# Placing the SBUF buffers of a two-block transformer kernel from both ends of the memory

## The chip, the core and the metric

The kernel runs on one core of one Trainium2 chip. The metric is the device time of the core in microseconds, from the first to the last instruction and what lies around them. Weights and inputs lie in HBM; the on-chip memory (SBUF) has 128 partitions, and every buffer of the kernel takes the same range of byte addresses in each of them. In this text an address is the byte offset within a partition.

## What is computed

Two residual blocks of two layers each act on x of 256 tokens by 1024 channels, all in float32. Cut to what matters:

```python
def first_block(x, ...):
    for l in range(DEPTH):                      # 2 layers
        h = rms_norm(x, attn_norm_g[l])
        pa, pb, pc = split(h @ w_in[l])         # RWKV-7, dilated and latent attention
        x = x + concat([ya, yb, yc]) @ w_out[l] # 1024 x 1024
        h = rms_norm(x, ffn_norm_g[l])
        x = x + (silu(h @ w_gate[l]) * (h @ w_up[l])) @ w_down[l]   # 1024 x 2816
    return rms_norm(x, final_norm_g)

def second_block(x, mem, ...):
    for l in range(DEPTH):                      # 2 layers
        proj = rms_norm_2(x, norm_g[l]) @ w_in[l]
        ...                                     # stick-breaking, MoBA, memory attention
        mkv = rms_norm_2(mem, mem_norm_g[l]) @ w_mem_kv[l]
        x = x + concat([o_sb, o_mb, o_mem]) @ w_out[l]
    return rms_norm_2(x, final_norm_g)
```

## The kernel before

The residual x is kept on chip with channels on partitions, as `x_res` (8 tiles of 128 channels by 256 tokens). Weights come from HBM as 132 chunks of 1 MB (128 partitions by 2048 floats), in the order of use, through the two halves of `w_raw`. Each product of a float32 weight with a float32 activation is made of three matmuls in the format float32r: the weight w is split into `w_hi` (rounded by ScalarE, L269) and `w_lo` = w minus w_hi (VectorE, L275), the activation in the same way (`act_hi`/`act_lo` for the normed x, `mixed_hi`/`mixed_lo` and `gated_hi`/`gated_lo` in the first block, `mem_hi`/`mem_lo` in the second), and the result is hi·HI + hi·LO + lo·HI. All these matmuls have a stationary operand of 128 columns and a moving operand of 256 columns; each loads its stationary operand anew. A chunk makes 48 of them, so there are 132 x 48 = 6336.

In nearly all of them the weight split is the stationary operand and the activation is the moving one, as in the gate and up projections of the feed-forward stage:

```python
TE.matmul(o, hi[:, w], HI[:, k, :], start=(k == 0 and x == 0), stop=False)
TE.matmul(o, hi[:, w], LO[:, k, :], start=False, stop=False)
last = TE.matmul(o, lo[:, w], HI[:, k, :], start=False, stop=(k == KT - 1 and x == 1))
```

Lines of the profile: L1120 to L1122 (input projections, first block), L1146 to L1148 (output projection, moving `mixed_*`), L1889 to L1891 (gate and up), L1911 to L1913 (down, moving `gated_*`), L2109 to L2111 (input projections, second block; in the two chunks of the memory's keys and values the activations are `mem_*`), L2141 to L2143 (output projection, moving `mem_*`). In some chunks the roles are turned, with w_hi or w_lo moving: L1125 to L1127 and L2114 to L2116.

By moving buffer: `act_*` or the weights with act stationary, 4320 matmuls; `gated_*` 528 in each layer; `mixed_*` 384; the memory's projections and the second block's output projection, with `mem_*`, 192 + 384 = 576.

The work runs in stages, one after the other: start, mixers of layer 0, feed-forward of layer 0, mixers of layer 1, feed-forward of layer 1, then the two layers of the second block. In each stage every engine has its own instruction list written out by hand; engines meet at semaphores. In the feed-forward stages TensorE's list is nearly only the matmuls above. In the mixer stages small matmuls of the attention and of the recurrence stand between the chunks.

SBUF buffers come from an allocator that stacks: each `K.sb(...)` takes the next free address, and leaving its context gives it back. Before the change all are stacked upwards from the low end, in the order of the calls; 16,512 bytes at the bottom are taken by the runtime and constants.

Of the kernel before, what the change touches and what calls it, by code (L numbers as in the profile page):

```python
# [28 lines left out]
fp32 = mybir.dt.float32  # L29
# [147 lines left out]
class Stream:  # L177
# [7 lines left out]
    def __init__(self, K):  # L185
        self.K, self.nc = K, K.nc
        raw = K.sb("w_raw", [P, 2, CHUNK])
# [105 lines left out]
class Kernel:  # L293
# [3 lines left out]
    def __init__(self, nc, ctx, io):  # L297
        self.nc, self.ctx, self.io = nc, ctx, io
        self.sems, self.total, self.base, self.named = {}, {}, {}, {}
        self.X = self.sb("x_res", [P, KT, T])  # L300
        self.HI = self.sb("act_hi", [P, KT, T], f32r)
        self.LO = self.sb("act_lo", [P, KT, T], f32r)
        self.PRMS = self.sb("prm", [P, WIDTH["prm"] + N_PRMS])
        self.st = Stream(self)
        self.SQ = self.sb("squares", [P, 3, 512])
        self.RSALL = self.sb("norm_rs", [P, T + NT])
        self.RSB, self.RS = self.RSALL[:, 0:T], self.RSALL[:, T:T + NT]
        self.cst_sb = {"both": self.sb("consts_both", [P, WIDTH["both"]]), "prm": self.PRMS}
# [2478 lines left out]
def program(nc, io, out):  # L2787
    with ExitStack() as ctx:
        K = Kernel(nc, ctx, io)
        GAINS = K.sb("gains", [P, KT])  # L2790
        block = ctx.enter_context(nc.Block())
        first, second = {}, {}
        with ExitStack() as c:
            norm = Norm(K, 0, 0, K.prm(Q_G, KT))
            first["rope_tables"] = K.sb("rope_tables", [P, 4, T], c=c)
            first["positions"] = K.sb("positions", [P, T], i32, c)[:, :]
# [4 lines left out]
            K.cst_sb["first"] = K.sb("consts_first", [P, WIDTH["first"]], c=c)  # L2801
# [13 lines left out]
        with ExitStack() as c:  # L2815
            K.cst_sb["second"] = K.sb("consts_second", [P, WIDTH["second"]], c=c)
            second["mem"] = K.sb("mem", [P, KT, T], c=c)[:, :, :]
            second["gates"] = K.sb("gates", [P, 8, T], c=c)
            second["mem_tokens"] = second["gates"].rearrange("p (t x) c -> p t (x c)", t=NT)
            second["mem_rs_row"] = K.sb("mem_rs_row", [P, T], c=c)  # L2820
            second["mem_ss"] = K.sb("mem_ss", [P, NT], c=c)
            second["mem_rs"] = K.sb("mem_rs", [P, NT], c=c)
            SQ2 = K.sb("scaled_squares", [P, 3, 512], c=c)
            R1 = K.sb("first_rs", [P, T + NT], c=c)
# [123 lines left out]
```

How the kernel before makes its waits and increments, by code:

```python
    def sync(self, name=None):  # L168
        name = name or self.own
        self.eng.wait_ge(self.K.sem(name), self.K.total[name])
# [43 lines left out]
    def split_quarter_hi(self, act, g, q):  # L214
        if q == 0:
            act.wait_ge(self.K.sem("quarters_in0" if g else "quarter_in"), 16)
        else:
            act.wait_ge(self.K.sem(f"quarters_in{q}"), 32)
        self.nc.scalar.activation(self.quarter(self.split[g][0], q), self.quarter(self.raw[g], q),
                                  ACT.Copy).then_inc(self.K.sem("quarter_hi"), 1)
# [1 line left out]
    def split_quarter_lo(self, dve, g, q):  # L222
        dve.wait_ge(self.K.sem("quarter_hi"), 2 * q + g + 1)
        hi, lo = (self.quarter(x, q) for x in self.split[g])
        self.nc.vector.tensor_tensor(lo, self.quarter(self.raw[g], q), hi.bitcast(fp32),
                                     ALU.subtract).then_inc(self.K.sem("quarter_lo"), 1)
# [1 line left out]
    def quarter_arrived(self, pe, g, q):  # L228
        pe.wait_ge(self.K.sem("quarter_lo"), 2 * q + g + 1)
# [12 lines left out]
    def load(self, sp, i):  # L242
        g = self.first + i
        if g >= len(self.src):
            return
        if g == 3:
            sp.wait_ge(self.K.sem("quarter_hi"), 2)
            sp.dma_start(self.raw_slot(g), self.src[g]).then_inc(self.K.sem("quarters_in0"), 16)
            return
        if g in (4, 5):
            sp.wait_ge(self.K.sem("quarter_hi"), g + 3)
            sp.wait_ge(self.K.sem("quarter_lo"), g + 3)
        elif g > 5:
            sp.wait_ge(self.hi_ready, self.ready(g - self.RAW, 1))
```

## Time and profile before

| | us |
|---|---|
| median of 3 runs | 969.79 (964.67 to 973.5) |
| profiled execution, its own time | 969.01 |
| profiled execution, span of its instructions | 967.2 |
| TensorE matmul busy | 937.9 (97%) |
| TensorE weight load busy | 886.4 (92%) |
| VectorE busy | 680.7 (70%) |
| ScalarE busy | 554.6 (57%) |
| DMA, mean rate over the span | 155 GB/s |

Matmuls overlap in the pipeline and their ends are modelled, so what matters of them is how far apart they start, not how long each is shown. The granted clock of TensorE is at 1.00 of 2.4 GHz in nearly every stretch.

### The profile page before, as it was taken

The numbers are of one execution on the slowest core, as the hardware profiler recorded it, in microseconds if no ns is written. First come the engines' busy times: TensorE is split into PE (matmuls) and PEld (weight loads), VectorE is DVE, ScalarE is ACT, GpSimd is POOL, SyncE is SP. The second block draws the span as 40 slices with busy tenths as digits, with TensorE's granted clock in tenths as the row PEclk, the third lists the DMA queues.
The fourth block names the chain that finished last, engine by engine and source line by source line (L and its number), as shares of the span: only waits on it lengthen the run. The fifth ranks groups of instructions, "written<-read, shape, count | busy, mean of one in ns | idle before, by whom it ended". The sixth has DMA issues, their size and how long they took to land.

```text
span 967.2 us, 20420 instructions
## 1 busy us (share of the span) xinstructions
PE 937.9 (97%) x8862; PEld 886.4 (92%) x8862; DVE 680.7 (70%) x972; ACT 554.6 (57%) x851; POOL 7.6 (1%) x12
## 2 busy tenths in 40 slices
PE   8899999999999999999999999999999999999996
PEld 7788799999999988878999999998899899999896
DVE  6898666866744679966776666348699677698674
ACT  6873466645443578355654444337487666486565
POOL 0000000000000001000000000000000000000000
PEclk9999999999999999999999999999999999999999
DMA  9341115565555433211466654554353335453241
GB/s 337 159 165 55 46 58 194 205 228 210 180 194 198 175 128 135 89 46 46 155 218 229 242 189 174 185 199 140 131 175 131 94 137 189 149 174 135 94 141 69
DMA packets 23145, 149.89 MB, mean 155 GB/s; under 512 B 2576, under 2 KB 2832, under 8 KB 6032
## 3 DMA queue, kind: packets, MB, share of 16 engines
q1 hardware_dynamic: 23056, 148.59, 43.2%
q8 instruction: 70, 1.15, 0.5%
q14 instruction: 19, 0.16, 0.0%
HBM read 147.26 MB, written 1.05 MB: 153 GB/s over the span
## 4 chain that ended last, share of the span: by engine, by line
PE 68%; DVE 18%; ACT 9%; issue 2%; DMA 1%; SPq 0%; DVEq 0%; ACTq 0%
PE bank L1889 8%; PE bank L1890 8%; PE bank L1891 8%; DVE w_lo L275 6%; PE bank L2109 4%; PE bank L1912 4%; PE bank L1911 4%; PE bank L1913 4%; ACT w_hi L269 3%; PE bank L2110 3%; PE bank L2111 3%; PE bank L2114 2%; PE bank L2116 2%; PE bank L2115 2%; ACT act_hi L372 1%
## 5 line engine op out<-in xcount | busy, mean ns | idle before, releaser
L275 DVE TENSOR_TENSOR w_lo<-w_raw,w_hi 128x1024 fp32r<-128x1024 f32 x256 | 306.4, 1225 | 108.5 <-ACT w_hi L269 107.6
L269 ACT ACTIVATE w_hi<-w_raw 128x1024 fp32r<-128x1024 f32 x256 | 259.5, 1053 | 209.0 <-PE bank L1891 103.3
L1889 PE MATMUL bank<-act_hi,w_hi 128*128 128x256 f32 x704 | 196.7, 279 | 1.6 <-DVE w_lo L275 1.0
L1890 PE MATMUL bank<-act_lo,w_hi 128*128 128x256 f32 x704 | 195.9, 278 | 0.0
L1891 PE MATMUL bank<-act_hi,w_lo 128*128 128x256 f32 x704 | 195.9, 278 | 0.0
L1889 PEld LDWEIGHTS bank<-act_hi,w_hi 128*128 128x128 f32 x704 | 133.5, 190 | 2.4 <-issue 1.4
L1890 PEld LDWEIGHTS bank<-act_lo,w_hi 128*128 128x128 f32 x704 | 132.2, 188 | 0.1
L1891 PEld LDWEIGHTS bank<-act_hi,w_lo 128*128 128x128 f32 x704 | 132.1, 188 | 0.0
L2109 PE MATMUL bank<-act_hi,w_hi 128*128 128x256 f32 x352 | 100.7, 286 | 3.9 <-DVE w_lo L275 2.4
L1912 PE MATMUL bank<-gated_lo,w_hi 128*128 128x256 f32 x352 | 98.7, 280 | 0.0
L1911 PE MATMUL bank<-gated_hi,w_hi 128*128 128x256 f32 x352 | 98.5, 280 | 0.0
L1913 PE MATMUL bank<-gated_hi,w_lo 128*128 128x256 f32 x352 | 98.5, 280 | 0.0
L2110 PE MATMUL bank<-act_lo,w_hi 128*128 128x256 f32 x352 | 97.8, 278 | 0.0
L2111 PE MATMUL bank<-act_hi,w_lo 128*128 128x256 f32 x352 | 97.8, 278 | 0.0
L1120 PE MATMUL bank<-act_hi,w_hi 128*128 128x256 f32 x256 | 75.0, 293 | 4.2 <-DVE w_lo L275 2.2
L2109 PEld LDWEIGHTS bank<-act_hi,w_hi 128*128 128x128 f32 x352 | 66.4, 189 | 6.9 <-DVE w_lo L275 3.4
L1122 PE MATMUL bank<-act_hi,w_lo 128*128 128x256 f32 x256 | 71.2, 278 | 0.0
L1121 PE MATMUL bank<-act_lo,w_hi 128*128 128x256 f32 x256 | 71.2, 278 | 0.0
L1911 PEld LDWEIGHTS bank<-gated_hi,w_hi 128*128 128x128 f32 x352 | 66.3, 188 | 0.0
L1912 PEld LDWEIGHTS bank<-gated_lo,w_hi 128*128 128x128 f32 x352 | 66.2, 188 | 0.0
L2110 PEld LDWEIGHTS bank<-act_lo,w_hi 128*128 128x128 f32 x352 | 66.2, 188 | 0.1
L2111 PEld LDWEIGHTS bank<-act_hi,w_lo 128*128 128x128 f32 x352 | 66.2, 188 | 0.0
(370 smaller groups left out, 1994.7 us busy)
## 6 DMA issues: line engine op xcount, KB each, us to landing
w_raw<-in_w_ffn SPq DMA_DIRECT2D x66, 1024.0 KB, 4.8
w_raw<-in_w_mix SPq DMA_DIRECT2D x62, 1024.0 KB, 4.9
small_w<-in_small SPq DMA_DIRECT2D x2, 1280.0 KB, 7.5
w_raw<-in_w_mix SPq DMA_DIRECT2D x8, 256.0 KB, 6.0
x_res<-in_x_channels SPq DMA_DIRECT2D x4, 256.0 KB, 5.6
probs<-in_w_mix SPq DMA_DIRECT2D x2, 512.0 KB, 7.5
probsT<-in_w_mix SPq DMA_DIRECT2D x1, 1024.0 KB, 10.2
mem<-in_mem_channels SPq DMA_DIRECT2D x1, 1024.0 KB, 7.4
```

Source lines behind the costliest of these rows:

```text
L269: self.nc.scalar.activation(hi, self.piece(self.raw_slot(g), p), ACT.Copy).then_inc(self.hi_ready, 1)
L275: self.nc.vector.tensor_tensor(lo, self.piece(self.raw_slot(g), p), hi.bitcast(fp32), ALU.subtract).then_inc(self.lo_ready, 1)
L1120: TE.matmul(o, hi[:, w], HI[:, k, :], start=(k == 0 and x == 0), stop=False)
L1889: TE.matmul(o, hi[:, w], HI[:, k, :], start=(k == 0 and x == 0), stop=False)
L1890: TE.matmul(o, hi[:, w], LO[:, k, :], start=False, stop=False)
L1891: last = TE.matmul(o, lo[:, w], HI[:, k, :], start=False, stop=(k == KT - 1 and x == 1))
L1911: TE.matmul(out, hi[:, w], GHI[:, k, :], start=(k == 0 and o % 2 == 0), stop=False)
L1912: TE.matmul(out, hi[:, w], GLO[:, k, :], start=False, stop=False)
L1913: last = TE.matmul(out, lo[:, w], GHI[:, k, :], start=False, stop=(k == FK - 1 and o % 2 == 1))
L2109: TE.matmul(o, hi[:, w], h[:, k, :], start=(k == 0 and x == 0), stop=False)
L2110: TE.matmul(o, hi[:, w], l[:, k, :], start=False, stop=False)
L2111: last = TE.matmul(o, lo[:, w], h[:, k, :], start=False, stop=(k == KT - 1 and x == 1))
```

## The change

The allocator is asked for two stacks: `K.sb(..., top=True)` takes its buffer from the high end of the memory downwards, all others from the low end upwards. On top go `x_res`, `prm`, `w_raw`, `squares`, `norm_rs`, `consts_*`, `gains`, `rope_tables`, `positions`, and of the second block `mem`, `gates`, `mem_rs_row`, `mem_ss`, `mem_rs`, `scaled_squares` and `first_rs`. At the low end stay `act_hi`/`act_lo`, `w_hi`/`w_lo`, `mixed_*`, `gated_*`, `mem_hi`/`mem_lo` and the buffers of the mixers.

```diff
-        raw = K.sb("w_raw", [P, 2, CHUNK])
+        raw = K.sb("w_raw", [P, 2, CHUNK], top=True)
         hi, lo = K.sb("w_hi", [P, 2, CHUNK], f32r), K.sb("w_lo", [P, 2, CHUNK], f32r)
...
-        self.X = self.sb("x_res", [P, KT, T])
         self.HI = self.sb("act_hi", [P, KT, T], f32r)
         self.LO = self.sb("act_lo", [P, KT, T], f32r)
-        self.PRMS = self.sb("prm", [P, WIDTH["prm"] + N_PRMS])
+        self.X = self.sb("x_res", [P, KT, T], top=True)
+        self.PRMS = self.sb("prm", [P, WIDTH["prm"] + N_PRMS], top=True)
         self.st = Stream(self)
-        self.SQ = self.sb("squares", [P, 3, 512])
-        self.RSALL = self.sb("norm_rs", [P, T + NT])
+        self.SQ = self.sb("squares", [P, 3, 512], top=True)
+        self.RSALL = self.sb("norm_rs", [P, T + NT], top=True)
...
-    def sb(self, name, shape, dt=fp32, c=None):
+    def sb(self, name, shape, dt=fp32, c=None, top=False):
...
-        return (c or self.ctx).enter_context(self.nc.sbuf_tensor(name, shape, dt))
+        return (c or self.ctx).enter_context(
+            self.nc.sbuf_tensor(name, shape, dt, side="right" if top else "left"))
...
-            K.cst_sb["second"] = K.sb("consts_second", [P, WIDTH["second"]], c=c)
-            second["mem"] = K.sb("mem", [P, KT, T], c=c)[:, :, :]
-            second["gates"] = K.sb("gates", [P, 8, T], c=c)
+            K.cst_sb["second"] = K.sb("consts_second", [P, WIDTH["second"]], c=c, top=True)
+            second["mem"] = K.sb("mem", [P, KT, T], c=c, top=True)[:, :, :]
+            second["gates"] = K.sb("gates", [P, 8, T], c=c, top=True)
```

No instruction is added, removed or moved: on every engine the list is the same, and so are all waits. Only addresses differ. The allocator aligns to 32 bytes; adding up the buffers' sizes gives these start addresses (all in bytes; the last two columns are the remainder on division by 512, before and after):

| buffer | size | before | after | mod 512 | mod 512 |
|---|---|---|---|---|---|
| act_hi | 8192 | 24704 | 16512 | 128 | 128 |
| act_lo | 8192 | 32896 | 24704 | 128 | 128 |
| w_hi | 16384 | 58560 | 32896 | 192 | 128 |
| w_lo | 16384 | 74944 | 49280 | 192 | 128 |
| mixed_hi | 8192 | 106240 | 65664 | 256 | 128 |
| mixed_lo | 8192 | 114432 | 73856 | 256 | 128 |
| gated_hi, layer 0 | 22528 | 131328 | 83072 | 256 | 128 |
| gated_lo, layer 0 | 22528 | 153856 | 105600 | 256 | 128 |
| gated_hi, layer 1 | 22528 | 131424 | 65664 | 352 | 128 |
| gated_lo, layer 1 | 22528 | 153952 | 88192 | 352 | 128 |
| mem_hi | 8192 | 131424 | 65664 | 352 | 128 |
| mem_lo | 8192 | 139616 | 73856 | 352 | 128 |
| w_raw | 16384 | 42176 | 203680 | 192 | 416 |
| x_res | 8192 | 16512 | 221152 | 128 | 480 |

Tiles within these buffers lie 512 or 1024 bytes apart, so they share the remainder.

## Rows read from the trace of the kernel before

**Rows 1.** Page, part 1: busy time, share of the span, instructions
```profile
PE 937.9 (97%) x8862; PEld 886.4 (92%) x8862; DVE 680.7 (70%) x972; ACT 554.6 (57%) x851; POOL 7.6 (1%) x12
```
**Rows 2.** Page, part 4: the chain that ended last, by engine
```profile
PE 68%; DVE 18%; ACT 9%; issue 2%; DMA 1%; SPq 0%; DVEq 0%; ACTq 0%
```
**Rows 3.** Windows: mixers 0, feed-forward 0 and 1, second block's layer 0
```profile
7.00:150.20 143.20, 135.73 (x1651) 120.01 (x1652) 113.97 (x201) 88.93 (x159) 3.68 (x4) 1.00 0.36 134
150.20:334.50 184.30, 183.51 (x1593) 183.08 (x1592) 115.96 (x128) 88.35 (x103) 0.00 (x0) 1.00 0.55 198
...
474.00:662.50 188.50, 187.71 (x1592) 187.29 (x1591) 115.52 (x127) 89.95 (x107) 0.00 (x0) 1.00 0.56 200
662.50:812.20 149.70, 144.98 (x1182) 135.46 (x1181) 117.11 (x176) 101.08 (x167) 0.00 (x0) 1.00 0.41 141
```
**Rows 4.** Timeline of PE (start us, us): gate/up, layer 0, 48 matmuls apart
```profile
261.43 0.28 PE L1889 MATMUL bank<-act_hi,w_hi 128*128 128x256 f32 x1
...
266.87 0.28 PE L1889 MATMUL bank<-act_hi,w_hi 128*128 128x256 f32 x1
```
**Rows 5.** Timeline of PE: gate/up, layer 1, 48 matmuls apart
```profile
537.74 0.28 PE L1889 MATMUL bank<-act_hi,w_hi 128*128 128x256 f32 x1
...
543.39 0.28 PE L1889 MATMUL bank<-act_hi,w_hi 128*128 128x256 f32 x1
```
**Rows 6.** Timeline of PE, gate/up to down, layer 0: 6, then 42 matmuls apart
```profile
271.63 0.28 PE L1889 MATMUL bank<-act_hi,w_hi 128*128 128x256 f32 x1
...
272.31 0.28 PE L1911 MATMUL bank<-gated_hi,w_hi 128*128 128x256 f32 x1
...
277.25 0.28 PE L1911 MATMUL bank<-gated_hi,w_hi 128*128 128x256 f32 x1
```
**Rows 7.** Timeline of PE: down, layer 1, 48 matmuls apart
```profile
624.84 0.28 PE L1911 MATMUL bank<-gated_hi,w_hi 128*128 128x256 f32 x1
...
630.54 0.28 PE L1911 MATMUL bank<-gated_hi,w_hi 128*128 128x256 f32 x1
```
**Rows 8.** Timeline of PE: output projection of the first block, 48 matmuls apart
```profile
139.12 0.28 PE L1148 MATMUL bank<-mixed_hi,w_lo 128*128 128x256 f32 x1
...
144.78 0.28 PE L1148 MATMUL bank<-mixed_hi,w_lo 128*128 128x256 f32 x1
```
**Rows 9.** Timeline of PE: output projection of the second block, 48 matmuls apart
```profile
950.17 0.28 PE L2141 MATMUL bank<-mem_hi,w_hi 128*128 128x256 f32 x1
...
955.88 0.28 PE L2141 MATMUL bank<-mem_hi,w_hi 128*128 128x256 f32 x1
```
**Rows 10.** Timeline of PE: weights moving, act stationary, 45 matmuls apart
```profile
706.19 0.28 PE L2114 MATMUL bank<-w_hi,act_hi 128*128 128x256 f32 x1
...
711.29 0.28 PE L2114 MATMUL bank<-w_hi,act_hi 128*128 128x256 f32 x1
```
**Rows 11.** Timeline of PE: weights moving, mem stationary, 24 matmuls apart
```profile
888.46 0.28 PE L2114 MATMUL bank<-w_hi,mem_hi 128*128 128x256 f32 x1
...
891.34 0.28 PE L2114 MATMUL bank<-w_hi,mem_hi 128*128 128x256 f32 x1
```
**Rows 12.** Groups by line, window 218.2:256.2 (gate/up, layer 0)
```profile
L1890 PE MATMUL bank<-act_lo,w_hi 128*128 128x256 f32 x113 | 31.2, 276 | 0.0
```
**Rows 13.** Groups by line, window 548.9:599.7 (gate/up, layer 1)
```profile
L1890 PE MATMUL bank<-act_lo,w_hi 128*128 128x256 f32 x145 | 40.7, 281 | 0.0
```
**Rows 14.** Page, part 5: three groups whose moving operand is act
```profile
L1891 PE MATMUL bank<-act_hi,w_lo 128*128 128x256 f32 x704 | 195.9, 278 | 0.0
...
L2111 PE MATMUL bank<-act_hi,w_lo 128*128 128x256 f32 x352 | 97.8, 278 | 0.0
...
L1122 PE MATMUL bank<-act_hi,w_lo 128*128 128x256 f32 x256 | 71.2, 278 | 0.0
```
**Rows 15.** Timeline of PE: 16 transposes in a row, other operands and form
```profile
932.47 1.91 PE L567 MATMUL bank<-consts_both,probs 128*128 128x128 f32 x16
```
**Rows 16.** Groups by line, VectorE: one shape at three places
```profile
L1933 DVE TENSOR_TENSOR gated<-up,gate 128x512 f32<-128x512 f32 x22 | 15.2, 692 | 1.2 <-ACT gate L1927 0.5
...
L394 DVE TENSOR_TENSOR squares<-squares 128x512 f32<-128x512 f32 x21 | 14.4, 688 | 0.7
```
**Rows 17.** Page, part 6: the weight chunks' transfers
```profile
w_raw<-in_w_ffn SPq DMA_DIRECT2D x66, 1024.0 KB, 4.8
```

More of the change, by code:

```diff
@@ L299, in __init__ @@
         self.sems, self.total, self.base, self.named = {}, {}, {}, {}
[L300 removed]
         self.HI = self.sb("act_hi", [P, KT, T], f32r)
         self.LO = self.sb("act_lo", [P, KT, T], f32r)
[L303 removed]
+        self.X = self.sb("x_res", [P, KT, T], top=True)
+        self.PRMS = self.sb("prm", [P, WIDTH["prm"] + N_PRMS], top=True)
         self.st = Stream(self)
[L305 to L306 removed]
+        self.SQ = self.sb("squares", [P, 3, 512], top=True)
+        self.RSALL = self.sb("norm_rs", [P, T + NT], top=True)
         self.RSB, self.RS = self.RSALL[:, 0:T], self.RSALL[:, T:T + NT]
[L308 removed]
+        self.cst_sb = {"both": self.sb("consts_both", [P, WIDTH["both"]], top=True), "prm": self.PRMS}
         self.PS = ctx.enter_context(nc.psum_tensor("bank", [P, 8 * 512], fp32))
         self.banks = [self.PS[:, 512 * i:512 * (i + 1)] for i in range(8)]
[L312 removed]
+    def sb(self, name, shape, dt=fp32, c=None, top=False):
         self.named[name] = self.named.get(name, -1) + 1
         name = f"{name}_{self.named[name]}" if c else name
[L315 removed]
+        return (c or self.ctx).enter_context(
+            self.nc.sbuf_tensor(name, shape, dt, side="right" if top else "left"))
     def sem(self, name):
@@ L2789, in program @@
         K = Kernel(nc, ctx, io)
-        GAINS = K.sb("gains", [P, KT])
+        GAINS = K.sb("gains", [P, KT], top=True)
         block = ctx.enter_context(nc.Block())
@@ L2794, in program @@
             norm = Norm(K, 0, 0, K.prm(Q_G, KT))
-            first["rope_tables"] = K.sb("rope_tables", [P, 4, T], c=c)
-            first["positions"] = K.sb("positions", [P, T], i32, c)[:, :]
+            first["rope_tables"] = K.sb("rope_tables", [P, 4, T], c=c, top=True)
+            first["positions"] = K.sb("positions", [P, T], i32, c=c, top=True)[:, :]
             with ExitStack() as shared:
@@ L2800, in program @@
             K.sb("small_w_end", [P, N_SMALL + 4 * T - 2 * KT * T], c=c)
-            K.cst_sb["first"] = K.sb("consts_first", [P, WIDTH["first"]], c=c)
+            K.cst_sb["first"] = K.sb("consts_first", [P, WIDTH["first"]], c=c, top=True)
             stage_start(K, block, norm, GAINS[:, :], first)
@@ L2815, in program @@
         with ExitStack() as c:
-            K.cst_sb["second"] = K.sb("consts_second", [P, WIDTH["second"]], c=c)
-            second["mem"] = K.sb("mem", [P, KT, T], c=c)[:, :, :]
-            second["gates"] = K.sb("gates", [P, 8, T], c=c)
+            K.cst_sb["second"] = K.sb("consts_second", [P, WIDTH["second"]], c=c, top=True)
+            second["mem"] = K.sb("mem", [P, KT, T], c=c, top=True)[:, :, :]
+            second["gates"] = K.sb("gates", [P, 8, T], c=c, top=True)
             second["mem_tokens"] = second["gates"].rearrange("p (t x) c -> p t (x c)", t=NT)
[L2820 to L2824, printed above, removed]
+            second["mem_rs_row"] = K.sb("mem_rs_row", [P, T], c=c, top=True)
+            second["mem_ss"] = K.sb("mem_ss", [P, NT], c=c, top=True)
+            second["mem_rs"] = K.sb("mem_rs", [P, NT], c=c, top=True)
+            SQ2 = K.sb("scaled_squares", [P, 3, 512], c=c, top=True)
+            R1 = K.sb("first_rs", [P, T + NT], c=c, top=True)
             chunk = DEPTH * (N_MIX1 + N_FFN)
```

## Prediction

> **What bounds the kernel now.** I began with the busy times: TensorE 97%, its weight loads 92%, VectorE 70%, ScalarE 57% [rows 1], and the chain that ended last is 68% TensorE [rows 2]. By stage, the two feed-forward stages (184.3 and 188.5 us) are filled to 99% by weight loads; the mixer stage shown has 84% and the second block's layer 90% [rows 3]. So what decides is how far apart TensorE's matmuls start. The change moves no instruction. It can act only if an address changes how long something takes, so the question put to the trace is: do equal matmuls on different buffers start at different distances?
>
> They do. All rows below are of one form (128 columns stationary, 256 moving), without a wait between them, at the full granted clock:
>
> - moving `act_*`, layer 0: 5.44 us for 48, or 113.3 ns [rows 4];
> - the same code on the same addresses in layer 1: 5.65 us for 48, 117.7 ns [rows 5];
> - moving `gated_*`, layer 0: 0.68 us for the 6 up to the border, 113.3 ns; 4.94 us for the 42 after it, 117.6 ns [rows 6]. The distance changes with the first matmul that reads `gated_hi`, with no wait there;
> - moving `mixed_*`: 5.66 us for 48, 117.9 ns [rows 8];
> - moving `gated_*` in layer 1, at a start 96 bytes off: 5.70 us for 48, 118.8 ns [rows 7];
> - moving `mem_*`: 5.71 us for 48, 119.0 ns [rows 9];
> - moving weights on stationary act: 5.10 us for 45, 113.3 ns [rows 10]; on stationary `mem_*`: 2.88 us for 24, 120.0 ns [rows 11].
>
> I read two things out of this. First, a stream can run in a fast beat (113.3) or a slow one (117.7) on the same addresses; something at its start picks one, and it keeps it. Second, `gated_*`, `mixed_*` and `mem_*` were never seen in the fast beat over a longer stretch, and `act_*` and the weights were. The buffers that can be fast all lie under 91,400; the others from 106,240 up. They also differ in the remainder by 512 (128 and 192 against 256 and 352), so the trace can't say whether height or remainder counts. The change puts every moving buffer at remainder 128, that of act, and all but a part of layer 0's `gated_*` (up to 128,128) under 111,000. By both readings it goes the same way.
>
> How often is act slow? A matmul is shown with 276 ns in the fast stretch [rows 12] and 281 in the slow one [rows 13]. The groups over the whole span give 195.9 / 704 = 278.3, 97.8 / 352 = 277.8 and 71.2 / 256 = 278.1 ns [rows 14], so 45%, 37% and 42% slow: I take 43%.
>
> **The change part by part.** Against 113.3 ns, what the 6336 matmuls now lose:
>
> 1. `gated_*`, layer 0: 528 x 4.4 = 2.3 us [rows 6].
> 2. `gated_*`, layer 1: 528 x 5.5 = 2.9 us [rows 7].
> 3. `mixed_*`: 384 x 4.6 = 1.8 us [rows 8].
> 4. `mem_*`, 576 x 5.7 = 3.3 us [rows 9].
> 5. act, slow 43% of the time: 4320 x 0.43 x 4.4 = 8.2 us [rows 5, 14].
>
> Together 18.5 us, 10.3 of it in the first four. The likeliest result is that after the change these four behave as act does, fast more than half of the time: they then still lose 2016 x 0.43 x 4.4 = 3.8 us, so 6.5 us are gained. Terms 1 to 3 lie in stretches that TensorE fills; term 4 lies in a stage filled to 90% [rows 3], where part is lost to waits for other engines. I take 0.9 of the whole: 5.9 us. Term 5 stays, as the beat is picked anew in each execution; it can differ by some 4 us a stage (22 chunks x 48 x 4.4 ns = 4.6 us), which is also the size of the spread of the three runs.
>
> Other engines' operations, with their operands at new places (`w_raw`, `x_res`, `squares`, constants): no trace shows them up there. One shape of VectorE takes 688 ns on `squares` (from 91,328) and 692 ns on `gate`/`up`/`gated` (from 176,384) [rows 16], 0.6% apart. On the 680.7 us of VectorE [rows 1] that is at most 4 us either way, and spread over an engine 30% idle: I take 0, with 1 us to both sides. The transfers into `w_raw` land in 4.8 us [rows 17] against 5.44 us in which a chunk is used up [rows 4]; they stay hidden. If they became slower by over 0.6 us each in the feed-forward stages, they would come to bound them; nothing in the trace ties their time to an address, so I price it at nothing.
>
> Sum on the profiled execution's own time: 969.0 - 5.9 = **963 us**. The median of the runs is 0.8 us above that execution, which I leave out.
>
> The Trainium skill speaks against any effect. "SBUF — State Buffer", in "Who interferes with whom", says that TensorE never waits on anyone, and "TensorE: Matmul & The Clock Gate", in its step on LDWEIGHTS, that loading the next weights takes no read bandwidth from the running matmul, since the two have ports of their own. By these rules equal matmuls take equal time wherever they read, and the time would stay at 969. The rows do not agree: 113.3 against 117.6 ns across a border with no wait [rows 6]. The second page also gives a spacing of columns over 2.4 GHz plus 2.5 ns, which would be 109.2 ns here; no stretch of these matmuls in this trace reaches it.
>
> **The rivals.**
>
> *All fast.* The remainders of the moving and the stationary operand become equal (128 and 128; now 128 against 192 for act), and if that takes away the meeting of the two read streams that makes the slow beat, all 6336 run at 113.3: 18.5 x 0.9 = 16.7 us gained, 952. For it: operands 32 bytes off a multiple of 64 are the slowest [rows 7, 9, 11], so finer alignment helps. Against it: no row shows that equal remainders are better than the present 64 bytes apart. It could go further: transposes of another form start 109 ns apart ((1.91 - 0.27) / 15) [rows 15]; with all at 109 the gain would be 6336 x 7.2 x 0.9 = 41 us, 928. That is the outermost bound.
>
> *Slower: the two streams meet in each matmul.* The same equal remainder can be the bad one. The stationary operand of the next matmul is loaded while the moving one is read; if both walk through the same part of the memory from the same remainder, each matmul pays. Price: the worst stretch seen, 120.0 ns [rows 11]. The mean now is 113.3 + 18.5 / 6336 = 116.2 ns, so (120.0 - 116.2) x 6336 x 0.9 = 22 us: 991. It decides from a mean above 116.2. A milder form is that only the slow beat is left: 4320 x 0.57 x 4.4 = 10.8 us lost, 528 x 1.1 + 576 x 1.3 = 1.3 us gained, times 0.9: 978.
>
> *No effect of the address.* Then `gated_*` and `mixed_*` were slow for another reason, such as the order in which output banks are written, and 969 stays. Against it: in the last two chunks of each such product the output stays on one half bank for 12 matmuls, longer than in gate and up, and a chunk of that kind ran in the slow beat too [rows 8].
>
> **How the numbers follow.** As act is now: 0.40, 963 (its own range 957 to 969). All fast: 0.31, 952, with a thin tail to 928. No effect: 0.11, 969. Slow beat only: 0.09, 978. Meeting in each matmul: 0.09, 991. About 1% (9.7 us) is what a measurement of this kernel can tell from no change. Faster by over 1% (under 960): all fast, and the lower edge of the first case: 0.35. Slower by over 1% (over 979.5): the last case and half of the one before: 0.15. Between: 0.50. The range is 946 to 983: it leaves out the last case and the tail of the second.
>
> **What would show each step.** In the profile after: L1911 to L1913, L1146 to L1148 and L2141 to L2143 have stretches of 48 matmuls in 5.44 us; their shown mean falls from 280 to about 278. Layer 1's feed-forward comes within one beat difference of layer 0's, since the 96-byte offset is gone. VectorE's L275 stays within 1% of 1225 ns and the raw chunks land in 4.8 us. The prediction is wrong if the spacing of `act_*` itself changes to a value that is neither 113.3 nor 117.7, because then the relation of the two operands, which I hold to be without effect, decides; or if L275 and L269 at their new places change by several per cent.

## The result and the profile after

| | before | after |
|---|---|---|
| median of 4 runs, us | 971.29 (964.67 to 973.5) | 984.83 (984.68 to 985.7) |
| profiled execution, span, us | 967.2 | 982.9 |

The ratio after to before is 1.0147, with a 95% interval from 1.0111 to 1.0183: slower by about 14 us. (One run more of the kernel before than in its own section: 972.79.) The forecast was 963, and 984.8 lies just outside the range of 946 to 983. One more thing has changed: the runs after lie within 1.0 us of each other, those of before within 8.8 us.

The page of the profile after: busy times, the chain that ended last, and four of its groups of instructions and transfers. From L378 of before on its line numbers are those of before plus 2.

```profile
PE 960.7 (98%) x8862; PEld 910.1 (93%) x8862; DVE 681.2 (69%) x972; ACT 554.5 (56%) x851; POOL 7.6 (1%) x12
...
PE 73%; DVE 15%; ACT 7%; issue 2%; DMA 1%; SPq 0%; DVEq 0%; ACTq 0%
...
L275 DVE TENSOR_TENSOR w_lo<-w_raw,w_hi 128x1024 fp32r<-128x1024 f32 x256 | 306.3, 1225 | 107.6 <-ACT w_hi L269 106.6
...
L1893 PE MATMUL bank<-act_hi,w_lo 128*128 128x256 f32 x704 | 199.2, 283 | 0.0
...
L1893 PEld LDWEIGHTS bank<-act_hi,w_lo 128*128 128x128 f32 x704 | 135.1, 192 | 0.0
...
w_raw<-in_w_ffn SPq DMA_DIRECT2D x66, 1024.0 KB, 4.8
```

Only TensorE has more busy time: 960.7 against 937.9 us for its matmuls, 910.1 against 886.4 us for its weight loads [rows 1]. VectorE (681.2 against 680.7) and ScalarE (554.5 against 554.6) stand still, the split of the weights reads `w_raw` from its new place in the same 1225 ns (the line of before is below), and its transfers land in the same 4.8 us [rows 17]. The chain has moved from VectorE to TensorE, 73% against 68% [rows 2]. So nothing shows a cost at the buffers that went to the top, and what costs is in the matmuls. L1893, with 199.2 us against 195.9, is shown with 283 ns, a duration that neither the fast nor the slow stretches of before have (276 and 281) [rows 12 to 14].

```profile
L275 DVE TENSOR_TENSOR w_lo<-w_raw,w_hi 128x1024 fp32r<-128x1024 f32 x256 | 306.4, 1225 | 108.5 <-ACT w_hi L269 107.6
```

By stage (mixers 0, feed-forward 0 and 1, the second block's layer 0; columns as in [rows 3]: the stretch and its length, the busy times of TensorE's matmuls, its weight loads, VectorE, ScalarE and GpSimd with their counts, the granted clock, the share of the DMA engines and GB/s):

```profile
7.00:150.90 143.90, 139.15 (x1651) 123.11 (x1650) 114.11 (x202) 88.60 (x158) 3.67 (x4) 0.99 0.36 133
150.90:342.60 191.70, 191.29 (x1591) 190.95 (x1591) 115.95 (x128) 88.29 (x103) 0.00 (x0) 1.00 0.52 191
482.40:674.20 191.80, 191.39 (x1593) 191.05 (x1592) 115.56 (x127) 89.91 (x107) 0.00 (x0) 1.00 0.54 196
674.20:825.90 151.70, 147.65 (x1180) 138.68 (x1180) 117.40 (x176) 101.06 (x167) 0.00 (x0) 1.00 0.40 140
```

Against [rows 3] the mixers are 0.7 us longer, the two feed-forward stages 7.4 and 3.3 us, the second block's layer 2.0 us. Before, the two feed-forward stages differed by 4.2 us; now they are equal. The granted clock is 1.00 in three of the four stages and 0.99 in the mixers, where before had 1.00 in all four, so the clock is not the reason.

The timeline of TensorE after, in pairs of rows 48 matmuls apart (the last pair 45): gate and up of layer 0, gate and up of layer 1, down of layer 1, output projection of the mixers 0, output projection at the very end, and a chunk of the second block in which `w_hi` moves and act is stationary.

```profile
261.12 0.28 PE L1891 MATMUL bank<-act_hi,w_hi 128*128 128x256 f32 x1
...
266.88 0.28 PE L1891 MATMUL bank<-act_hi,w_hi 128*128 128x256 f32 x1
...
537.82 0.28 PE L1893 MATMUL bank<-act_hi,w_lo 128*128 128x256 f32 x1
...
543.58 0.28 PE L1893 MATMUL bank<-act_hi,w_lo 128*128 128x256 f32 x1
...
624.82 0.28 PE L1914 MATMUL bank<-gated_lo,w_hi 128*128 128x256 f32 x1
...
630.58 0.28 PE L1914 MATMUL bank<-gated_lo,w_hi 128*128 128x256 f32 x1
...
139.82 0.28 PE L1150 MATMUL bank<-mixed_hi,w_lo 128*128 128x256 f32 x1
...
145.58 0.28 PE L1150 MATMUL bank<-mixed_hi,w_lo 128*128 128x256 f32 x1
...
964.94 0.28 PE L2145 MATMUL bank<-mem_hi,w_lo 128*128 128x256 f32 x1
...
970.70 0.28 PE L2145 MATMUL bank<-mem_hi,w_lo 128*128 128x256 f32 x1
...
718.83 0.28 PE L2116 MATMUL bank<-w_hi,act_hi 128*128 128x256 f32 x1
...
724.23 0.28 PE L2116 MATMUL bank<-w_hi,act_hi 128*128 128x256 f32 x1
```

Five times 5.76 us for 48, and 5.40 us for 45: 120.0 ns in each. Before, the same places had 113.3 or 117.7 (act), 118.8, 117.9, 119.0 and 113.3 [rows 4, 5, 7 to 10]. Everything runs in one beat, whatever the moving buffer, and it is the spacing that of the streams shown before only the worst had [rows 11].

### The profile page after: what moved, and what is told of

Its sections match the earlier page's. It is cut to its first block, busy times and chain, and to the rows that moved or that the text cites. A ratio compares the mean times of both kernels' runs of the same rounds, so it can differ in the third digit from the quotient of the medians.

```text
span 982.9 us, 20420 instructions
## 1 busy us (share of the span) xinstructions
PE 960.7 (98%) x8862; PEld 910.1 (93%) x8862; DVE 681.2 (69%) x972; ACT 554.5 (56%) x851; POOL 7.6 (1%) x12
## 4 chain that ended last, share of the span: by engine, by line
PE 73%; DVE 15%; ACT 7%; issue 2%; DMA 1%; SPq 0%; DVEq 0%; ACTq 0%
PE bank L1891 8%; PE bank L1892 8%; PE bank L1893 8%; DVE w_lo L275 5%; PE bank L2111 4%; PE bank L2112 4%; PE bank L2113 4%; PE bank L1915 4%; PE bank L1914 4%; PE bank L1913 4%; ACT w_hi L269 3%; PE bank L2116 2%; PE bank L2118 2%; PE bank L2117 2%; PE bank L569 1%
## 5 line engine op out<-in xcount | busy, mean ns | idle before, releaser
L269 ACT ACTIVATE w_hi<-w_raw 128x1024 fp32r<-128x1024 f32 x256 | 259.2, 1052 | 218.0 <-PE bank L1893 115.6
L275 DVE TENSOR_TENSOR w_lo<-w_raw,w_hi 128x1024 fp32r<-128x1024 f32 x256 | 306.3, 1225 | 107.6 <-ACT w_hi L269 106.6
L1891 PE MATMUL bank<-act_hi,w_hi 128*128 128x256 f32 x704 | 199.9, 284 | 0.8 <-DVE w_lo L275 0.8
L1892 PE MATMUL bank<-act_lo,w_hi 128*128 128x256 f32 x704 | 199.2, 283 | 0.0
L1893 PE MATMUL bank<-act_hi,w_lo 128*128 128x256 f32 x704 | 199.2, 283 | 0.0
L1891 PEld LDWEIGHTS bank<-act_hi,w_hi 128*128 128x128 f32 x704 | 135.1, 192 | 1.5 <-issue 1.2
L1892 PEld LDWEIGHTS bank<-act_lo,w_hi 128*128 128x128 f32 x704 | 135.1, 192 | 0.1
L1893 PEld LDWEIGHTS bank<-act_hi,w_lo 128*128 128x128 f32 x704 | 135.1, 192 | 0.0
L2111 PE MATMUL bank<-act_hi,w_hi 128*128 128x256 f32 x352 | 102.1, 290 | 3.2 <-DVE w_lo L275 2.2
L2112 PE MATMUL bank<-act_lo,w_hi 128*128 128x256 f32 x352 | 99.5, 283 | 0.0
L2113 PE MATMUL bank<-act_hi,w_lo 128*128 128x256 f32 x352 | 99.5, 283 | 0.0
L1122 PE MATMUL bank<-act_hi,w_hi 128*128 128x256 f32 x256 | 76.3, 298 | 2.1 <-DVE w_lo L275 1.4
L2111 PEld LDWEIGHTS bank<-act_hi,w_hi 128*128 128x128 f32 x352 | 67.3, 191 | 6.0 <-DVE w_lo L275 3.3
L1123 PE MATMUL bank<-act_lo,w_hi 128*128 128x256 f32 x256 | 72.4, 283 | 0.0
L1124 PE MATMUL bank<-act_hi,w_lo 128*128 128x256 f32 x256 | 72.3, 283 | 0.0
L1915 PEld LDWEIGHTS bank<-gated_hi,w_lo 128*128 128x128 f32 x352 | 67.6, 192 | 0.0
L2112 PEld LDWEIGHTS bank<-act_lo,w_hi 128*128 128x128 f32 x352 | 67.4, 191 | 0.1
```

The source lines that it names most:

```text
L269: self.nc.scalar.activation(hi, self.piece(self.raw_slot(g), p), ACT.Copy).then_inc(self.hi_ready, 1)
L275: self.nc.vector.tensor_tensor(lo, self.piece(self.raw_slot(g), p), hi.bitcast(fp32), ALU.subtract).then_inc(self.lo_ready, 1)
L1915: last = TE.matmul(out, lo[:, w], GHI[:, k, :], start=False, stop=(k == FK - 1 and o % 2 == 1))
L2111: TE.matmul(o, hi[:, w], h[:, k, :], start=(k == 0 and x == 0), stop=False)
L2112: TE.matmul(o, hi[:, w], l[:, k, :], start=False, stop=False)
L2113: last = TE.matmul(o, lo[:, w], h[:, k, :], start=False, stop=(k == KT - 1 and x == 1))
```

## The experiments

Two words are needed in what follows. The **distance** of a matmul is the address of its moving operand minus that of its stationary one, modulo 256 bytes. I write "act on w" for act moving and the weights stationary. Before, act on w has distance 192, `gated_*` of layer 0 and `mixed_*` 64, `gated_*` of layer 1 and `mem_*` 160, weights moving on act 64, weights moving on `mem_*` 96. After, all have 0. Wherever a spacing is given, it is the mean time from start to start in a stretch without a wait; where the single steps alternate, it moves by 0.1 or 0.2 ns with the stretch chosen. For the whole kernel I also use the **loss**: the sum over its unbroken pairs of such matmuls of what their spacing has above 113.33 ns. It is 18.2 us before and 40.7 us after.

### The new places with the old remainders, and the old places with equal remainders

First kernel: the changed one, with gaps that give every operand back its old remainder by 512 while it stays at its new height.

```diff
         self.LO = self.sb("act_lo", [P, KT, T], f32r)
...
+        self.sb("gap_w", [P, 16])
         self.st = Stream(self)
+        self.sb("gap_moving", [P, 16])
...
+            K.sb("gap_second", [P, 24], c=c)
             K.cst_sb["second"] = K.sb("consts_second", [P, WIDTH["second"]], c=c, top=True)
```

> The changed kernel with three gaps (64 bytes ahead of w_hi, 64 bytes behind w_lo, 96 bytes ahead of the second block's buffers), so that every buffer stays at its new place from both ends, but the weight splits and moving operands have the remainders by 512 that they had before (act 128, w 192, mixed and gated of layer 0 256, gated of layer 1 and mem 352). Theory R (the remainder between moving and stationary operand sets the spacing of the matmuls): back to the time of before, 965 to 973 us, act in beats of 113.3 or 117.7 ns, gated 117.7 and 118.7. Theory P (the new places themselves cost, by height or through w_raw, x_res and the constants at the top): stays at 985, spacing 120.0 everywhere.

Measured: 970.63 us (10 runs) against 969.16 for the kernel before (13 runs), ratio 1.0002 [0.997, 1.0033]; loss 16.5 us. The rows of its groups:

```profile
L1894 PE MATMUL bank<-act_lo,w_hi 128*128 128x256 f32 x704 | 195.9, 278 | 0.0
L1895 PE MATMUL bank<-act_hi,w_lo 128*128 128x256 f32 x704 | 195.9, 278 | 0.0
```

195.9 us is the number of the kernel before [rows 14]. Gaps of 64, 64 and 96 bytes in memory that nothing uses give the whole 14 us back.

Second kernel: the one before, all stacked from the low end, with `prm` behind the weight buffers and gaps, so that every operand has the same remainder.

```diff
-        self.PRMS = self.sb("prm", [P, WIDTH["prm"] + N_PRMS])
         self.st = Stream(self)
+        self.PRMS = self.sb("prm", [P, WIDTH["prm"] + N_PRMS])
...
+            K.sb("gap_first", [P, 96], c=c)
...
+            K.sb("gap_second", [P, 72], c=c)
```

> The kernel before with prm moved behind w_lo and two gaps (384 and 288 bytes), so that all buffers stay stacked from the low end within a few hundred bytes of their old places, but act, w, mixed, gated and mem all have the remainder 128 by 512. Theory R: 983 to 987 us, spacing 120.0 ns for all 6336 matmuls. Theory P: 965 to 973 us, spacings as before.

Measured: 985.81 us (985.36 to 985.98, 4 runs), ratio 1.0158 [1.0102, 1.0214]; loss 40.7 us, the very number of after, and 120.0 ns in every stream.

```profile
L1890 PE MATMUL bank<-act_lo,w_hi 128*128 128x256 f32 x704 | 199.2, 283 | 0.0
L1891 PE MATMUL bank<-act_hi,w_lo 128*128 128x256 f32 x704 | 199.2, 283 | 0.0
```

With that the result is explained down to the low bits of the addresses: the remainders are all of it, and height and the two stacks show no effect (to 0.3%, the interval of the first pair; the last pair of kernels below agrees to 0.1 us). What it is in the remainders, the next two kernels ask.

### Matmuls alone: the distance, then the height

A kernel of nothing but the matmuls of a chunk (output: a copy of x). All operands lie in one buffer `big`. A group is 48 matmuls in the order of the gate and up projections; three groups are run at each distance, and TensorE waits for ScalarE between them. LO has the remainder of HI, w_lo that of w_hi.

```python
for m, st in CONFIGS:                   # addresses of HI and w_hi
    ...
    for r in range(GROUPS):
        ...
        for k in range(8):
            for x in range(2):
                ...                     # the slices of big
                TE.matmul(o, hi, HI, ...)
                TE.matmul(o, hi, LO, ...)
                last = TE.matmul(o, lo, HI, ...)
        g += 1
        last.then_inc(s["pe"], 1)
        pe.wait_ge(s["go"], g)
```

> Not the reference's work: only float32r matmuls (128 columns stationary, 256 moving, the order hi.HI, hi.LO, lo.HI of the kernel) on one big buffer, 24 settings of the distance moving minus stationary, three runs of 48 matmuls for each with a wait between them; the output is a copy of x. Both operands lie under 70,000. Distances modulo 1024: 0, 16, 32, 48, 64, 96, ... 480, 512, 576, 768, 960, then 0 and 64 again. Theory R: distance 0 gives 120.0 ns in all three runs; 64 and 448 (960) give 113.3 or 117.7 by run; distances that are not a multiple of 64 give 118 to 121; a multiple of 512 is as 0, and I have no forecast for 128, 256 and 384 (if the period is 128, all three as 0). Theory P: no spacing depends on the distance, all of 113 to 118 as both operands are low.

Measured (ns; where groups at one distance differ, all values seen; the first group of all, whose first matmuls start 213 ns apart, is counted in none of these kernels):

| distance | spacing | distance | spacing |
|---|---|---|---|
| 0, 256, 512, 768 | 120.0 | 128, 384 | 118.7, once 120.0 |
| 16 | 117.3 | 160 | 117.3 to 118.7 |
| 32 | 116.7 to 117.8 | 192, 448, 960 | 113.3 |
| 48 | 116.7 | 224, 480 | 118.3 |
| 64, 320, 576 | 117.8, 117.8, 113.3 | 288 | 116.7 to 117.8 |
| 96, 352 | 120.0 | 416 | 117.3 to 118.7 |

The first two rows below have distance 0, the last two distance 192; each pair is 30 matmuls apart:

```profile
43.71 0.28 PE L76 MATMUL bank<-big 128*128 128x256 f32 x1
...
47.31 0.28 PE L76 MATMUL bank<-big 128*128 128x256 f32 x1
...
194.31 0.28 PE L76 MATMUL bank<-big 128*128 128x256 f32 x1
...
197.71 0.28 PE L76 MATMUL bank<-big 128*128 128x256 f32 x1
```

3.60 us is 120.0 ns each, 3.40 us is 113.3 ns. The pattern repeats after 256 bytes. It also fits the streams of the trace of before: act at 192 in the fast beat (the slow one was not seen here, but is below), weights moving on act at 64 with 113.3 [rows 10], `gated_*` and `mixed_*` at 64 with 117.6 and 117.9, `mem_*` at 160 with 119.0, weights moving on `mem_*` at 96 with 120.0 [rows 6, 8, 9, 11]. What the slow beat is, it doesn't say.

> As the other measuring kernel, not the reference's work. Distances 0, 64 and 960 modulo 1024, each with moving/stationary operand near 17,500/37,000, 106,600/58,500, 131,200/58,500, 131,200/169,000 and 37,000/131,200; then distance 64 and 960 with the moving operand at remainders 0, 64, 160 and 256 by 1024; last the old place and remainder of gated (131,328 against 58,560). Theory R: the three groups of five differ, within a group all are alike: 120.0 for distance 0 and 113.3 or 117.7 for the others, wherever they lie; the absolute remainder is without effect except 160. Theory P with height: moving operands over 100,000 run at 117.7 or more, those at 17,500 reach 113.3, whatever the distance.

The same kernel at five places for both operands (moving at 17,536, 36,992, 106,624 and twice 131,200; stationary between 36,992 and 169,088) for each of three distances, then other remainders of the moving operand at distances 64 and 192. Measured: distance 0 gives 120.0 at all five places; 64 gives 117.8, 117.8, 113.3 at all five; 192 gives 113.3 at all five. Moving operands at remainders 0, 64 and 160 by 256 show no other values either. So, as long as LO has the remainder of HI and w_lo that of w_hi, only the distance of the two counts, and neither the height nor where one of them lies by itself. At distance 64 the group at 113.3 is nearly always the same: the third of its setting in 13 of the 14 settings of both kernels, always behind ScalarE's copy of 76 columns, and another group only once. So the start has a say in it.

### Every moving activation at distance 192

If 192 is the fast distance, `gated_*`, `mixed_*` and `mem_*` should get it as well: once with the old places, once with the new. (The matmuls with weights moving then all have 64.)

```diff
+            K.sb("gap_first", [P, 32], c=c)
...
+            K.sb("gap_second", [P, 8], c=c)
```

> The kernel before with two gaps only (128 bytes ahead of rope_tables, 32 bytes ahead of consts_second): act and w stay where they were, and mixed, gated and mem get a distance to w of -64 modulo 256, the one that act has. The measuring kernel ran this distance at 113.3 ns in all its runs, in every place. Theory R: mixed, gated and mem mostly at 113.3 instead of 117.7 to 119.0 ns; at most 10.3 us gained, less where act's slow beat (43% of its time before) is carried over: 959 to 966 us against 969. Theory P (high operands are slow): no change.

```diff
+        self.sb("gap_w", [P, 16])
         self.st = Stream(self)
+        self.sb("gap_moving", [P, 48])
```

> The changed kernel with two gaps (64 bytes ahead of w_hi, 192 bytes behind w_lo), so that all moving operands have the distance -64 modulo 256 to w, at the new places. Theory R: the same time as the kernel with this distance at the old places, within 0.5%, 959 to 966 us: 20 us less than the changed kernel as it is. If low operands or the top places give anything of their own, the two differ.

Measured: 966.22 (12 runs), ratio 0.9986 [0.9959, 1.0013], and 970.97 (12 runs), ratio 1.0027 [1.0003, 1.0051]. I had expected 959 to 966. Neither is a gain over the kernel before. But the single runs come in steps. Old places: 960.65, 961.34, 961.51; six from 965.6 to 967.2 and two near 968; 972.44. New places: three from 965.3 to 966.9, nine from 970.5 to 971.9. The two profiled executions lie on different steps. Old places (the two feed-forward stages of a 961.34 run):

```profile
150.60:333.00 182.40, 181.11 (x1592) 180.69 (x1591) 116.16 (x128) 88.24 (x103) 0.00 (x0) 1.00 0.55 200
472.10:654.90 182.80, 181.58 (x1592) 181.16 (x1591) 115.33 (x127) 89.21 (x106) 0.00 (x0) 1.00 0.56 206
```

The mean spacing is 113.5 and 113.8 ns in these stages, `gated_*` included. New places (the groups of a 971.79 run):

```profile
L1895 PE MATMUL bank<-act_hi,w_lo 128*128 128x256 f32 x704 | 197.4, 280 | 0.0
L1894 PE MATMUL bank<-act_lo,w_hi 128*128 128x256 f32 x704 | 197.3, 280 | 0.0
...
L1916 PE MATMUL bank<-gated_lo,w_hi 128*128 128x256 f32 x352 | 98.9, 281 | 0.0
```

Here both stages run at 117.4 ns on the average, 188.5 us each. At distance 192 a stage can have either beat for nearly its whole length, and that is worth 6 us a stage. The first kernel of the experiments speaks for a new draw in each execution: it has the remainders of before, but in its trace layer 0's feed-forward stage is the slow one (188.1 us) and layer 1's the fast one (184.1), the other way round from [rows 3]. The steps of some 5 us between runs are of this size, so this is very likely where the spread of the kernel before comes from; only one execution of each kernel has a trace. That the average over runs gains so little fits too: in both traces the buffers that came to 192 are fast or slow together with act.

The traces also show where the beat changes. The feed-forward stages of these four kernels (before, its remainders at the new places, and the two here) are interrupted at the same three points: a wait after 36 matmuls, a few small matmuls of the norm (L406 and L407 of before) after 144, and a wait of 0.8 us after 192. In all eight stages the beat of act changes at these points and nowhere else. The fourth chunk, between the last two, is slow in all eight; the beat that follows the third point, fast in four and slow in four, lasts to the end of act.

### What picks the beat?

Three kernels of matmuls alone. The first takes distances close to 192 and starts after a wait or after float32 matmuls:

> Measuring kernel, not the reference's work. Distances 192, 176, 184, 188, 196, 200, 208, 64, 128 and 0 modulo 1024, eight groups of 48 matmuls each: four after waits of different length, then four with 0 to 3 float32 matmuls of 256 columns ahead and no wait. It asks what puts a stream with distance 192 into the slow beat, as act has it in 43% of its time in the kernel before. If the start decides: some of the eight groups of 192 run at 117.7. If the neighbours that stand ahead without a wait decide, only the last three do. Between 176 and 208 I expect 113.3 at 192 alone, as 160 and 224 gave 117 to 118.5.

Measured: 192 gives 113.3 in six of seven groups and 117.8 in one (after one float32 matmul). 188 and 184 give 118.3 to 118.4, 196 gives 119.1 to 119.9, 200 and 208 between 117.6 and 118.4, 176 gives 118.7. Four bytes to either side cost 5 ns or more. And the slow beat can be entered at the very distance that can be fast.

The second starts groups at distance 192 in many ways, and puts one or a few other matmuls between two groups without a wait (`kick`: float32r ones at another distance; `plain`: float32 ones):

```python
elif step[0] == "kick":
    for q in range(step[1]):
        last = TE.matmul(PS[:, 3584:3840], big[:, b:b + 128], big[:, a:a + 256], start=True, stop=True)
```

> Measuring kernel, not the reference's work. All groups of 48 at distance 192. For each of 14 insertions (nothing; 1 or 3 single float32r matmuls at distance 64, 0 or 128 or one 32 bytes off; 1, 2 or 3 float32 matmuls of 256 columns, 1 or 2 of 128, 1 or 4 of 64): a group that starts after a wait (fast so far), the insertion, a group; then one float32 matmul of 256 columns (which led into the slow beat in the run before), a group, the insertion, a group. If the beat is a phase that the stream keeps, the insertion can move it: some insertion turns slow into fast, and the same may turn fast into slow. If the beat is set by something else at that moment, the same insertion gives no regular answer. From the kernel before, where act turned fast at once after mixed (distance 64), I expect the float32r matmuls at distance 64 to do it.

Measured: both beats come after either kind of start. An insertion often flips the beat, in either direction: one float32 matmul of 128 columns made a slow stretch fast and a fast one slow; one float32r matmul at distance 64, of which I had expected that it leaves the beat slow, left one stretch slow and made the next fast. Three float32 matmuls of 256 columns gave the fast beat both times, one float32r matmul at distance 0 the slow one both times; with two trials each that proves nothing. No rule for the start came out.

The third leaves the starts and changes the three kinds of matmul of a triple apart from each other. Its distances are given in the order HI on w_hi, LO on w_hi, HI on w_lo:

> Measuring kernel, not the reference's work. Twelve combinations of the distances HI minus w_hi, LO minus w_lo and HI minus w_lo, seven groups each, four after waits and three after float32 matmuls. Which distance counts: if the load of the next stationary operand meets the running matmul's moving read, then HI - w_hi and LO - w_lo count (the next load under hi.HI is w_hi, under hi.LO w_lo, under lo.HI the next w_hi), and HI - w_lo does not: 192/192/x runs as 192/192/192 for every x, 192/0/192 is slower by a third of 6.7 ns or more, 64/64/192 is as 64. If a matmul's own stationary operand counts instead, 192/192/0 is slower.

Measured, in seven groups each: 192/192/192 either beat; 192/64/192 117.8; 192/0/192 117.8 to 119.4; 192/128/192 118.8; 192/64/64 121; 192/128/0 119.2 to 119.4, once 120.0; 192/0/128 118.5 to 118.6; 64/64/192 118.9 four times and 113.3 three times; 64/192/192, 64/192/64 and 192/0/64 117.8. One stood out: **192/192/64** settled at 113.3 after all seven starts, within some 15 matmuls. In it HI and LO have the same remainder, w_hi lies 64 bytes above it and w_lo 64 bytes below it (by 256). That a matmul's own distance sets its spacing, as I had held after the first four kernels, is refuted by this: with one distance in three at 64, one arrangement (192/64/192) never came under 117.8 and the other (192/192/64) settled at 113.3 every time, and 192/64/64 takes 121, more than either distance ever takes alone (117.8). The operands of the neighbours count too.

### All arrangements in steps of 64 bytes, and the best one in the kernel

```python
# addresses of HI, LO, w_hi, w_lo; over HI: the others each at 0, 64, 128, 192 more; two groups each
('g', 16512, 24960, 41088, 57728), ('wait', 8), ('plain', 1, 256), ('g', 16512, 24960, 41088, 57728), ...
```

> Measuring kernel, not the reference's work. All 64 combinations of the remainders of LO, w_hi and w_lo against HI (0, 64, 128, 192 by 256 each), two groups of 48 matmuls each, one after a wait and one after a float32 matmul. Which relations count was mixed up in the run on pairs, since LO moved with w_lo. Theory R with the running matmul's own stationary operand without effect: the result depends on HI - w_hi, LO - w_lo and HI - w_hi alone. If own operands count too, LO - w_hi and HI - w_lo matter. Anything under 113.3 ns would be a new best; the combination 0, 64, 192 (LO, w_hi, w_lo over HI) is to be 113.3 in both starts.

Measured, of 64 arrangements (LO, w_hi, w_lo over HI): (0, 64, 192) is the only one with 113.3 in both of its groups. (0, 64, 64), which is all at distance 192, gives 117.8 once and 113.3 once. The next are (128, 64, 128), (0, 192, 128) and (128, 192, 128) at 115.6; about half lie between 117.6 and 118. (0, 0, 0), the arrangement of the changed kernel, gives 120.0, the worst (128, 64, 192) 120.9. None is below 113.3. Rows of (0, 64, 192), 30 matmuls apart:

```profile
123.51 0.28 PE L86 MATMUL bank<-big 128*128 128x256 f32 x1
...
126.91 0.28 PE L86 MATMUL bank<-big 128*128 128x256 f32 x1
```

The kernel before with this arrangement:

```diff
-        hi, lo = K.sb("w_hi", [P, 2, CHUNK], f32r), K.sb("w_lo", [P, 2, CHUNK], f32r)
+        hi = K.sb("w_hi", [P, 2, CHUNK], f32r)
+        K.sb("gap_lo", [P, 32])
+        lo = K.sb("w_lo", [P, 2, CHUNK], f32r)
...
+            K.sb("gap_second", [P, 40], c=c)
```

> The kernel before with two gaps (128 bytes between w_hi and w_lo, 160 bytes ahead of consts_second): all moving operands have the remainder 128 by 256, w_hi 192, w_lo 64. The measuring kernel ran this combination at 113.3 ns in all its seven starts, those that led into the slow beat with w_lo at 192 too. If it holds here: all 6336 matmuls near 113.3 ns, the shown mean 276 ns on L1889 to L1891 and L1911 to L1913, single runs within 1 us of each other instead of the steps of 5 us, 952 to 957 us. If the slow beat comes from something else in the real kernel: 961 to 971 in steps as with w_lo at 192.

Measured: 959.97 us (959.7 to 960.79, 8 runs) against 965.33 (13 runs), ratio 0.9933 [0.9906, 0.9959]. The loss falls to 4.1 us, and the spread from 10 us to 1 us.

```profile
L1893 PE MATMUL bank<-act_hi,w_lo 128*128 128x256 f32 x704 | 194.6, 276 | 0.0
L1892 PE MATMUL bank<-act_lo,w_hi 128*128 128x256 f32 x704 | 194.6, 276 | 0.0
...
L1914 PE MATMUL bank<-gated_lo,w_hi 128*128 128x256 f32 x352 | 97.3, 276 | 0.0
```

276 ns over all 704 matmuls is the fast beat's number of [rows 12], now for gate and up of both layers, and `gated_*` has it too. I had expected 952 to 957. The spacing fell nearly as far as I had said, but the time didn't follow, as the table of stages in the next section shows. In the chunks with the roles turned, where the arrangement is another one, the spacing is 117.7.

Last, the changed kernel with the same arrangement:

```diff
+        self.sb("gap_w", [P, 16])
         self.st = Stream(self)         # with the 32 floats between w_hi and w_lo
+        self.sb("gap_moving", [P, 16])
```

> The changed kernel with three gaps (64 bytes ahead of w_hi, 128 between w_hi and w_lo, 64 behind w_lo), so that it has the same remainders as the fastest kernel at the old places: moving operands 128, w_hi 192, w_lo 64 by 256. If the remainders are all that the change did to the time, this lies within 0.3% of that kernel, 958 to 962 us, again with single runs within 1 us of each other. If the new places cost or give something that the earlier pairs of runs could not show for their steps of 5 us, it differs by over 3 us.

Measured: 959.86 us (959.2 to 960.68, 6 runs) against 969.39 (11 runs), ratio 0.9909 [0.989, 0.9927]. Its busy times, and down of layer 1, 48 matmuls apart (5.44 us, 113.3 ns):

```profile
PE 926.3 (97%) x8862; PEld 874.0 (91%) x8862; DVE 680.6 (71%) x972; ACT 555.4 (58%) x851; POOL 7.6 (1%) x12
```

```profile
622.05 0.28 PE L1917 MATMUL bank<-gated_hi,w_hi 128*128 128x256 f32 x1
...
627.49 0.28 PE L1917 MATMUL bank<-gated_hi,w_hi 128*128 128x256 f32 x1
```

Two stacks or one, both kernels run in 960 us. 64 bytes ahead of the weight buffers, 128 between them and 64 behind them turn the change from 1.5% slower into 0.9% faster than the kernel before.

## Why the prediction was wrong

**The step that failed** is the reading of what the streams of before have in common: "The change puts every moving buffer at remainder 128, that of act ... By both readings it goes the same way." I looked at the moving operand alone, its height and its own remainder, and held "the relation of the two operands" to be without effect. The prediction's own sign of being wrong, a spacing of act that is neither 113.3 nor 117.7, came: it is 120.0. The rows allowed the other reading: act on w, `gated_*` on w, `mem_*` on w and w on `mem_*` each had another distance and another spacing, and in [rows 11] the very buffers `w_hi` and `mem_hi`, with their roles turned, took 120.0 instead of 119.0 [rows 9]. Remainder 128 was kept for act, but w moved from 192 to 128, so act's distance went from 192, which can be fast, to 0, which never is. Both kernels at the start of the experiments show it: new heights with old distances cost nothing, old heights with distance 0 cost 16 us. In the sum this is the 5.9 us taken as gained; the profiled executions lost 15.7 us (969.0 to 984.7).

**The rival "the two streams meet in each matmul"** described what happened, at a chance of 0.09. Its spacing of 120.0 was right in every stream. Its price was off by one term, the share that reaches the end. The spacing loss rose from 18.2 to 40.7 us, by 22.5 us (the rival had 24 before its factor), and the span by 15.7: a share of 0.70 where I took 0.9. The stages show where it went (us, from the first weight matmul of a stage to that of the next, in the last column to the last weight matmul; the mean spacing in brackets, in ns):

| | mixers 0 | feed-fwd 0 | mixers 1 | feed-fwd 1 | second, 0 | second, 1 |
|---|---|---|---|---|---|---|
| before | 143.2 (116.4) | 184.3 (115.0) | 139.5 (116.2) | 188.6 (117.7) | 149.6 (115.9) | 144.7 (116.5) |
| after | 143.9 (119.7) | 191.7 (120.0) | 139.8 (119.8) | 191.7 (120.0) | 151.7 (119.8) | 146.5 (119.9) |
| before with 192/192/64 | 143.4 (114.4) | 182.4 (113.4) | 139.0 (114.3) | 182.5 (113.4) | 149.9 (114.8) | 144.4 (114.7) |

A feed-forward stage of 33 chunks passes its spacing on almost whole: 1584 x 5.0 ns = 7.9 us of spacing and 7.4 us of time in layer 0. In the mixers of layer 0 624 x 3.4 ns = 2.1 us of spacing made 0.7 us of time, in those of layer 1 2.2 us made 0.3, and in the second block some 55% came through. Downwards it is less still: from before to 192/192/64 the two feed-forward stages gain 8.0 us together, the other four stages 0.3 us, although their spacing fell by 1.1 to 2.0 ns, some 5 us in all. There other engines end the waits, and a faster TensorE only waits longer for them: in the second block's layer 0 its waits for VectorE's results (`w_lo`, `act_lo`, `squares` and the like) add up to 4.1 us after the change, 4.8 before and 5.7 with 192/192/64. The busy share of a stage (84% and 90% in [rows 3]) was no measure of that.

**The terms of the sum.** The loss against 113.3 was well counted: 18.5 us predicted, 18.2 measured over all matmuls of the profiled execution. That terms 1 to 4 (`gated_*`, `mixed_*`, `mem_*`) could be won was right as well, and `gated_*` did reach 113.3, but not by this change. Term 5, act's beat drawn anew in each execution, was right in kind and size for the kernel before: the two executions with its remainders have their slow stage 4 us above the fast one, in opposite order. That it would stay was wrong. After the change there is only one beat, and the spread of 1.0 us fits that.

**The other rivals.** "No effect of the address" is refuted by the matmuls alone and by the kernels with equal remainders; the order of the output banks was not the reason, since `gated_*` runs at 113.3 with the same order. "All fast" rested on equal remainders being the good ones; they are nearly the worst, and what makes the streams with the weights stationary fast is 64 bytes apart upwards and downwards. What I drew from the rules of the Trainium skill ("SBUF — State Buffer", "Who interferes with whom", and the LDWEIGHTS step of "TensorE: Matmul & The Clock Gate"), that equal matmuls take equal time wherever they read, doesn't hold for these streams: 113.3 against 120.0 ns with nothing changed but low bits of addresses, in a kernel in which no other engine works at the time. The first rule is about other engines, and nothing here speaks against that. The second says that loading the next weights takes nothing from the running matmul's reads; that their addresses count together speaks against it, but no run shows what in the memory or the engine makes the meeting.

**What I priced at nothing** stayed at nothing: L275 at 1225 ns and the landing of `w_raw` at 4.8 us, above, and VectorE's 692 and 687 ns on the shapes of [rows 16] (692 and 688).

**What stays open.** Why the pattern repeats after 256 bytes, why a stream at distance 192 has two beats and what at an interruption picks one, and why 192/192/64 alone always settles in the fast one. The runs show it, and none explains it. An arrangement for the chunks with the roles turned (117.7 in the best kernel) was not tried; they lie in the mixers and the second block, where the table gives little hope for it.

## What to carry to other kernels

When TensorE's matmuls stand back to back, measure how far apart they start in each stream before and after anything is moved in SBUF: the low bits of the addresses of moving and stationary operands, taken together, were worth 2.5% here (960 against 985 us), so fix them on purpose, with an arrangement tried in a small kernel of matmuls alone. Price a change of spacing stage by stage, since here only the stages that weight loads fill to 99% passed it on almost whole. A run-to-run spread in steps can be a beat that is picked at a start, and an arrangement can remove it.

## What the runs showed of the hardware

- Float32r matmuls of 128 stationary by 256 moving columns, each with a stationary operand of its own, start between 113.3 and 121 ns apart at the full granted clock, by where the low eight bits of their operands' addresses lie to each other. With all at one distance (moving minus stationary, modulo 256 bytes) it is 120.0 at 0, 113.3 or 117.8 at 64 and 192, and 116.7 to 120.0 at the others tried. Neither the height (five places) nor the remainder of all operands together made a difference.
- The best distance is sharp: 192 can have 113.3, while 188 never had less than 118.3 and 196 never less than 119.1.
- At distance 192 (and in part at 64) the same stream has two stable beats, 113.3 and 117.8 ns. A single inserted matmul can flip it, in both directions; in the feed-forward stages of the whole kernels act's beat changed only at waits and at the norm's matmuls between.
- With w_hi 64 bytes above and w_lo 64 bytes below the remainder of the moving operands, 48-matmul groups settled at 113.3 after all nine starts tried (seven and two), and the feed-forward stages of two whole kernels averaged 113.4.
- VectorE and ScalarE showed no effect of moving part of their operands to the other end of the memory: busy times within 0.1% (681.2 against 680.7 and 554.5 against 554.6 us). The chunks into `w_raw` landed in 4.8 us at either end.
